# One scatter for two experts, one-hot transposes in other PSUM banks, and the low parts of the mixing weights on VectorE

## What is computed

```python
p = h @ w_in                      # pool | conv a | conv b | q k v | z | decay, beta | gates
y_pool = pool_mixer(...)          # causal means over 2, 4, 8, 16 tokens, mapped 128 -> 256 per group
y_conv = silu(layer_norm(causal_depthwise(glu, w_dw) + b_dw)) @ w_conv_out      # 31 taps
y_dn   = gated_rmsnorm(gated_delta_chunked(q, k, v, g, beta, S0), z) @ w_dn_out # q, k, v: 4 taps, silu
mixed  = gates0 * y_pool + gates1 * y_conv + gates2 * y_dn
x = layer_norm(ALPHA * x + mixed @ w_out)
x = layer_norm(ALPHA * x + ffn(x))                  # layer 0: swiglu; layer 1:
    vals, idx = lax.top_k(x @ w_router + b_router, 2); wts = softmax(vals)
    out = sum over e of gate[:, e] * swiglu(x, wg[e], wu[e], wd[e])
```

## Time and profile before

| what | us |
|---|---|
| median of 3 runs | 1764.94 (1764.79 to 1766.91) |
| the profiled execution, whole | 1761.52 |
| its span, first to last instruction | 1759.7 |
| mixing stage of layer 0, to the layer norm | about 5 to 453 |
| dense feed-forward | about 468 to 710 |
| mixing stage of layer 1 | about 724 to 1178 |
| experts, to the last add | about 1207 to 1736 |

### The profile page before, as it was taken

One profiled execution on the slowest core, in us unless ns is written; L12 is line 12 of the kernel. 1 busy time (PEld: TensorE's weight loads), 2 busy tenths in 40 slices (PEclk: granted clock), 3 DMA queues, 4 the chain that ended last, 5 costly groups with the idle time before them and its releaser, 6 DMA issues.

```text
span 1759.7 us, 22898 instructions
## 1 busy us (share of the span) xinstructions
PE 1555.0 (88%) x8707; PEld 1361.5 (77%) x8707; DVE 1153.0 (66%) x1564; ACT 813.4 (46%) x1352; POOL 828.7 (47%) x414
## 2 busy tenths in 40 slices
PE   7798888899799999688988898888999899899885
PEld 6687787787699999567888788765878778778774
DVE  6779786557611011686979844855787688688774
ACT  4544443532333243353534434322666566567653
POOL 4457565426376667343756642440343244234332
PEclk9999899989899999898998997996999999999987
DMA  5222223312355453322222332233687588588771
GB/s 230 96 96 75 70 72 101 144 48 90 121 165 160 130 159 106 123 72 96 77 85 81 95 127 72 72 133 114 217 324 291 199 308 304 200 301 306 262 253 41
DMA packets 57523, 264.66 MB, mean 150 GB/s; under 512 B 9024, under 2 KB 9664, under 8 KB 48448
## 3 DMA queue, kind: packets, MB, share of 16 engines
q1 hardware_dynamic: 57408, 263.11, 43.3%
HBM read 254.54 MB, written 8.54 MB: 150 GB/s over the span
## 4 chain that ended last, share of the span: by engine, by line
PE 47%; DVE 29%; POOL 10%; issue 9%; ACT 4%; DMA 1%; POOLq 0%; ACTq 0%; DVEq 0%; SPq 0%
POOL fl L528 7%; PE ps L1320 6%; PE ps L1321 6%; PE ps L1322 6%; DVE cacc L1565 6%; PE ps L1025 5%; PE ps L1026 4%; PE ps L1027 4%; PE ps L1293 3%; DVE ml L1907 2%; DVE kT L1473 2%; DVE qT L1473 2%; DVE pw L1538 1%; DVE G L1810 1%; POOL ml L592 1%
## 5 line engine op out<-in xcount | busy, mean ns | idle before, releaser
L548 POOL TENSOR_TENSOR Wl<-raw,Wh 128x1024 fp32r<-128x1024 f32 x138 | 344.5, 2500 | 351.3 <-ACT Wh L619 351.0
L1025 PE MATMUL ps<-Xh,Wl 128*128 128x320 f32 x976 | 335.0, 343 | 49.1 <-POOL Wl L548 31.4
L1907 DVE TENSOR_TENSOR ml<-mraw,mh 128x1408 fp32r<-128x1408 f32 (+1 forms) x160 | 299.4, 1892 | 105.1 <-ACT mh L910 104.5
L592 POOL TENSOR_TENSOR ml<-mraw,mh 128x1408 fp32r<-128x1408 f32 (+1 forms) x56 | 184.9, 3302 | 363.5 <-ACT mh L910 363.5
L910 ACT ACTIVATE mh<-mraw 128x1408 fp32r<-128x1408 f32 (+1 forms) x216 | 268.4, 1252 | 112.5 <-PE ps L1322 109.1
L1026 PE MATMUL ps<-Xl,Wh 128*128 128x320 f32 x976 | 314.1, 322 | 0.0
L1027 PE MATMUL ps<-Xh,Wh 128*128 128x320 f32 x976 | 313.8, 322 | 0.0
L1025 PEld LDWEIGHTS ps<-Xh,Wl 128*128 128x128 f32 x976 | 195.5, 200 | 76.3 <-POOL Wl L548 43.1
L528 POOL TENSOR_TENSOR fl<-fraw,fh 128x1024 fp32r<-128x1024 f32 (+1 forms) x60 | 158.8, 2652 | 88.2 <-ACT fh L857 88.2
L1026 PEld LDWEIGHTS ps<-Xl,Wh 128*128 128x128 f32 x976 | 195.6, 200 | 0.3
L1027 PEld LDWEIGHTS ps<-Xh,Wh 128*128 128x128 f32 x976 | 194.6, 199 | 0.0
(11 more groups left out here) (336 smaller groups left out, 3151.7 us busy)
## 6 DMA issues: line engine op xcount, KB each, us to landing
mraw<-w_moe SPq DMA_DIRECT2D x128, 704.0 KB, 6.3
raw<-w_mix SPq DMA_DIRECT2D x68, 1024.0 KB, 4.9
mraw<-w_moe SPq DMA_DIRECT2D x88, 512.0 KB, 4.3
fraw<-w_ffn SPq DMA_DIRECT2D x44, 512.0 KB, 3.5
fraw<-w_ffn SPq DMA_DIRECT2D x16, 704.0 KB, 4.0
Ss<-st_delta SPq DMA_DIRECT2D x2, 2048.0 KB, 9.1
o_delta_s<-Ss SPq DMA_DIRECT2D x8, 512.0 KB, 2.6
X<-x SPq DMA_DIRECT2D x2, 640.0 KB, 5.7
```

The source lines that it names most:

```text
L548: pool.tensor_tensor(Wl[:, n % 3, :], raw[:, b % 3, u % 2, :], Wh[:, n % 3, :].bitcast(f32), ALU.subtract).then_inc(w_lo, 1)
L592: pool.tensor_tensor(ml[:, n % MS, 0:w], mraw[:, n % MRAW, 0:w], mh[:, n % MS, 0:w].bitcast(f32), ALU.subtract).then_inc(m_lop, 1)
L1025: pe.matmul(out, wl, xh, start=start, stop=False)
L1907: dve.tensor_tensor(ml[:, n % MS, 0:w], mraw[:, n % MRAW, 0:w], mh[:, n % MS, 0:w].bitcast(f32), ALU.subtract).then_inc(m_lod, 1)
```

## The change

Three things are changed.

1. The low part `Wl` of every mixing unit is made by DVE (`wrest`) in place of POOL (`rest`), at the same place of the list `STEPS`. For the first two units of layer 1 both halves stand ahead of the layer norm's own work, and the first two units of layer 0 stand between the splits of X. POOL keeps its share of the taps, the sums and the other low parts.
2. The results of experts 2p and 2p + 1 stay in two sets of `yh` and `yl`, and one scatter adds both in PSUM (four matmuls per block in place of two), spread over tiles 3 to 10 of expert 2p + 2. DVE adds 32 blocks in place of 64.
3. The slot weights of a pair are made once, after tile 2 of the even expert, in PS[3], and both one-hot transposes after tile 2 of the odd expert, in PS[3] and PS[4], the banks of the up tiles. PE waits for their copies by ACT ahead of tile 8.

```diff
 # experts, ACT
-                    act.wait_ge(m_ptc, e + 1)
+                    if e >= 2:
+                        act.wait_ge(m_sc, 8 * (e // 2))
...
-                    if i == 7 + SCAT:
-                        act.wait_ge(m_pt, e + 1)
-                        act.activation(gslot[:, :], PS[6][:, T:T + 1], ACT.Copy)
-                        act.activation(PT[:, :], PS[6][:, 0:T], ACT.Copy).then_inc(m_ptc, 1)
+                    if i == 4 and e % 2 == 0:
+                        act.wait_ge(m_gs, e // 2 + 1)
+                        act.activation(gslot[:, e:e + 2], PS[3][:, 0:2], ACT.Copy).then_inc(m_ptc, 1)
+                    if i == 4 and e % 2:
+                        act.wait_ge(m_pt, e // 2 + 1)
+                        for j in range(2):
+                            act.activation(PT[:, j, :], PS[3 + j][:, 0:T], ACT.Copy).then_inc(m_ptc, 1)
 # experts, PE
+                def slots(e):
+                    if e:
+                        pe.wait_ge(m_tlo, 3 * e)
+                    pe.wait_ge(m_p, e + 2)
...
+                def places_turned(e):
+                    pe.wait_ge(m_tlo, 3 * e)
...
-                def scatter(e, m):
+                def scatter(pair, m):
                     if m == 0:
-                        pe.wait_ge(m_ylo, 2 * e + 2)
-                        pe.wait_ge(m_ptc, e + 1)
-                    else:
-                        pe.wait_ge(m_acc, e * 8 + max(m - 1, 0))
+                        pe.wait_ge(m_ylo, 4 * pair + 4)
+                        pe.wait_ge(m_ptc, 3 * pair + 3)
+                    elif m > 1:
+                        pe.wait_ge(m_acc, 8 * pair + m - 1)
                     c = slice(128 * m, 128 * m + 128)
-                    pe.matmul(PS[6 + m % 2][:, 0:T], yl[:, c], PT[:, :], start=True, stop=False)
-                    pe.matmul(PS[6 + m % 2][:, 0:T], yh[:, c], PT[:, :], start=False, stop=True).then_inc(m_sc, 1)
+                    o = PS[6 + m % 2][:, 0:T]
+                    for j in range(2):
+                        pe.matmul(o, yl[j][:, c], PT[:, j, :], start=(j == 0), stop=False)
+                        ins = pe.matmul(o, yh[j][:, c], PT[:, j, :], start=False, stop=(j == 1))
+                    ins.then_inc(m_sc, 1)
...
                         else:
+                            if k == MG:
+                                pe.wait_ge(m_ptc, 3 * (e // 2) + (3 if e % 2 else 1))
                             wide(e * MN + k, PS[3:6], FUNIT, *fed(k - MG), k == MG, False)
-                        if k >= SCAT and e:
-                            scatter(e - 1, k - SCAT)
-
-                    pe.wait_ge(m_p, 2 * (e // 2) + 2)
-                    pe.wait_ge(xt_dve, 6)
-                    if e:
-                        pe.wait_ge(m_acc, e * 8)
...
+                        if k == 2:
+                            if e % 2:
+                                places_turned(e)
+                            else:
+                                slots(e)
+                        if k >= SCAT and e and e % 2 == 0:
+                            scatter(e // 2 - 1, k - SCAT)
 # experts, DVE
-                    if SCAT <= i < SCAT + 8 and e:
-                        add(e - 1, i - SCAT)
+                    if SCAT <= i < SCAT + 8 and e and e % 2 == 0:
+                        add(e // 2 - 1, i - SCAT)
 # mixing, POOL
-            def rest(n):
...
-                rest(l * NU)
-                rest(l * NU + 1)
...
-                        if p == 0 and u < U_WO + 6:
-                            rest(l * NU + u + 2)
 # mixing, DVE
             def ln(l, w):
...
+                if w == 2:
+                    wrest((l + 1) * NU)
+                    wrest((l + 1) * NU + 1)
...
+            def wrest(n):
...
+                dve.wait_ge(w_hi, n + 1)
+                dve.tensor_tensor(Wl[:, n % 3, :], raw[:, b % 3, u % 2, :],
+                                  Wh[:, n % 3, :].bitcast(f32), ALU.subtract).then_inc(w_lo, 1)
...
             def part(l, u, p):
+                if p == 0 and u < U_WO + 6:
+                    wrest(l * NU + u + 2)
```

More of the change, by code:

```diff
@@ L115, in build @@
             ("gate", [128, 3, NE + 1], f32), ("posm", [128, 3, NE + 1], f32),
-            ("gslot", [128, 1], f32), ("flag", [128, 1], mybir.dt.int32))
+            ("gslot", [128, NE], f32), ("flag", [128, 1], mybir.dt.int32), ("warm", [1, 1], f32))
+        SQAT = sum(size(s) for s in ([1, NCON], [1, DEPTH, NPAR], [1, KT, T], [1, KT, T], [1, KT, T], [1, 3, 2, UNIT],
+                                     [1, 3, UNIT], [1, 3, UNIT], [1, KT, 8]))
         (G, EXT) = lay(TOP, ("G", [128, 24, T], f32))
@@ L568, in _ @@
                 for kind, x in STEPS:
-                    if kind == "part":
-                        u, p = x
-                        if p == 0 and u < U_WO + 6:
-                            rest(l * NU + u + 2)
-                    elif kind == "ptap":
+                    if kind == "ptap":
                         tap(l, *x)
@@ L593, in _ @@
                                            mh[:, n % MS, 0:w].bitcast(f32), ALU.subtract).then_inc(m_lop, 1)
-                    sums(m_acc, 8 * (NE - 1), asum, KT - 1)
+                    sums(m_acc, 4 * NE - 8, asum, KT - 1)
                     with pool.If(overflow(pool)):
@@ L735, in ln @@
                 src = (None, X, acc)[w]
-                act.activation(std[0:1, 0:1], C("ones", 1), ACT.Sqrt)
+                if w == 2:
+                    head((l + 1) * NU)
+                    head((l + 1) * NU + 1)
+                act.activation(warm[:, :], C("ones", 1), ACT.Sqrt)
                 for m in range(k):
@@ L748, in ln @@
                     return
[L749 to L752, removed]
+                if w == 1 and l == 0:
                     fhead(0, 0)
                     fhead(0, 1)
-                else:
+                elif w == 1:
                     mhead(0)
@@ L939, in y_head @@
                     act.wait_ge(m_done, (e + 1) * MN)
-                    act.wait_ge(m_ptc, e + 1)
+                    if e >= 2:
+                        act.wait_ge(m_sc, 8 * (e // 2))
                     for c in range(2):
-                        act.activation(yh[:, 512 * c:512 * c + 512], PS[6 + c][:, :], ACT.Copy, scale=gslot[:, 0:1])\
+                        act.activation(yh[e % 2][:, 512 * c:512 * c + 512], PS[6 + c][:, :], ACT.Copy, scale=gslot[:, e:e + 1])\
                             .then_inc(m_yhi, 1)
@@ L1367, in experts @@
                         pe.wait_ge(m_p, 2 * (e // 2) + 4)
+                        pe.wait_ge(m_ylo, 2 * e)
+                        pe.wait_ge(m_acc, 8 * (e // 2))
                         gather_next(e, 0)
[L1369 removed]
                         gather_next(e, 1)
@@ L1389, in experts @@
                 for m in range(8):
-                    scatter(NE - 1, m)
+                    scatter(NE // 2 - 1, m)
             def ffn(l):
@@ L1940, in y_rest, with add @@
                         s = slice(512 * c, 512 * c + 512)
-                        dve.scalar_tensor_tensor(out=yl[:, s], in0=PS[6 + c][:, :], scalar=gslot[:, 0:1],
-                                                 in1=yh[:, s].bitcast(f32), op0=ALU.mult, op1=ALU.subtract).then_inc(m_ylo, 1)
-                def add(e, m):
-                    dve.wait_ge(m_sc, e * 8 + (m + 1))
+                        dve.scalar_tensor_tensor(out=yl[e % 2][:, s], in0=PS[6 + c][:, :], scalar=gslot[:, e:e + 1],
+                                                 in1=yh[e % 2][:, s].bitcast(f32), op0=ALU.mult, op1=ALU.subtract).then_inc(m_ylo, 1)
+                def add(pair, m):
+                    dve.wait_ge(m_sc, 8 * pair + m + 1)
                     dve.tensor_tensor(acc[:, m, :], acc[:, m, :], PS[6 + m % 2][:, 0:T], ALU.add).then_inc(m_acc, 1)
@@ L1993, in experts @@
                 for m in range(8):
-                    add(NE - 1, m)
-                dve.wait_ge(m_acc, 8 * NE)
+                    add(NE // 2 - 1, m)
+                dve.wait_ge(m_acc, 4 * NE)
             for m in range(KT):
@@ L1999, in _ @@
                 dve.tensor_tensor(Xl[:, m, :], X[:, m, :], Xh[:, m, :].bitcast(f32), ALU.subtract).then_inc(split_lo, 1)
+                if m % 4 == 3:
+                    wrest(m // 4)
             dve.wait_ge(par_in, 16)
```

54 lines of the change are left out of this document (28 added, 26 removed).

## The result

The changed kernel takes 1664.46 us (median of 4, 1656.22 to 1667.15) beside 1765.93 us for the kernel before on the same chip: a ratio of 0.9416, 95% interval 0.9383 to 0.9448. The profiled executions differ by 94.3 us in span (1759.7 and 1665.4).

What follows compares the result with a forecast made beforehand. No single engine was taken to bound the kernel: POOL's `Wl` holds DVE, and late adds pause PE and halve its clock. Mixing stages -39 and experts -35 sum to -74, a median of 1691 us, range 1665 to 1727.

Steps and rivals of the forecast that it cites:

- What bounds the kernel: Whole kernel: pace passes between engines; PE's idle time could give 205 us; POOL's `Wl` stops DVE some 2 us.
- q, k, v units: Units at each layer's start: without the hold PE becomes the slower engine; -11 us in layer 0, -14 in layer 1.
- First delta steps: Units 14, 15 and 17: `Wl` and a wait for `Wh` stand ahead of steps PE needs; +1 us per layer.
- Woven part: 100 to 300 us in layer 0: `Wl` cost 33, waits for `Wh` at half, holds -49; -3 us per layer.
- Branches: End of the branches, 340 to 450 us: holds of 18.9 us go, 16 `Wl` cost 18; -5 us per layer.
- Experts: Pair scatter and moved transposes: -25 waits, -20 half clock, +8 remaining pauses, +2 tail; -35 us.
- the tail: End of the experts: the last pair's 8 blocks of four matmuls at half clock end some 2 us later.
- the residual: Even experts: `ml` may still delay an `add` before a block; three pauses of the longest kind, 8 us.
- A: Rival, woven part: waits for `Wh` block DVE while delta steps queue; +12 per layer, not -3; 1721 us; chance 0.15.
- B: Rival, experts: they keep their idle, paced by DVE, loads or two-expert blocks; -5, not -35; 1721 us; chance 0.11.
- C: Rival, mixing stages: `Wl` on DVE and POOL's taps hold each other up, mixing gains nothing; 1730 us; chance 0.06.
- D: Rival, slower: from the woven part on each `Wl` and `Wh` wait lies on the path; 1780 us; chance 0.04.

Runs made afterwards that it cites:

- experiment 6: The changed kernel, but DVE makes `Wl` only for units 0 to 13 of each layer and POOL makes the other 55: 1694.9 us.
- experiment 2: The kernel before with `Wl` made by DVE and the high parts ahead of the norm, experts unchanged: 1713.15 us.
- experiment 3: The changed kernel without pairs: one scatter per expert, 64 adds, each transpose after the expert's third tile in PS[4]: 1663.28 us, ratio 0.9422.
- experiment 4: The changed kernel with the pair scatter, but slot weights and transposes behind tile 10 in PS[6] and PS[7]: 1683.4 us.
- experiment 5: The changed kernel with one wait put back: in experts 2, 4 and 6 PE waits behind tile 10 for the pair's last add: 1670.27 us.

## Why the prediction was off

**What bounds the kernel.** Right. The hold of DVE by POOL's `Wl`, the last add ahead of the transposes, and the half clock behind a pause were the three causes, and each came up in the experiments. The size was not: the median came 26.5 us under the forecast of 1691. 20.3 of them are the difference of the profiled spans (94.3 measured, 74 forecast), 13 in the experts and 7 in the mixing stages. The other 6 are scatter: the profiled execution of the kernel before lay 3.4 us under its median, that of the changed kernel 2.7 above its own. The 7 of the mixing stages are small by luck, since the woven parts gave 17 us more than forecast and the start of layer 1 and the branches 10 less.

**q, k, v units.** Layer 0: -11 forecast, -10.6 measured. PE is the slower engine, as forecast: most of its units take 4.35 to 4.67 us, and it has no wait over 0.2 us between them up to 69.6. The activations were not 4.3 to 4.5 us apart, though. Two steps took 8.94 and 8.58, in which DVE waited for ACT, and six took 3.74, DVE's own time (3.8 was worked out), with which it caught up. Layer 1: -14 forecast, -10.2 measured. The units gave 9.3, and the start about 1 in place of 4.5. The two operations on X fell from 4.04 to 1.01 us as forecast, but the norm's `std` by ACT ahead of them was only 18.6 us earlier in a kernel that was 21.2 ahead at the end of layer 0's branches; the two `Wl` that stand before it on DVE are 3.0 us of work there. And the third tile came no sooner, because ACT's high part of it waits for its load:

```profile
715.06 1.06 ACT L610 ACTIVATE Wh<-raw 128x1024 fp32r<-128x1024 f32 x1 [6.44 <-DMA raw<-w_mix]
```

It stood at 736.04 before, behind 6.07 us of the same wait, so it moved by 21.0 us. PE still waits 3.8 us for that tile's `Wl`, where it waited 4.60. No run tested an earlier load.

**First delta steps.** +1 forecast in each layer; +2.5 measured in layer 0 and -0.1 in layer 1.

**Woven part, the first step that failed.** The step is "I count a wait at half: -3 per layer" (by its own terms, 33 + 12 - 49, it would be -4). The part gave 13 us in layer 0 and 10 in layer 1. Units 20 to 52 of layer 0 in the kernel before:

```profile
119.50:338.30 218.80, 189.45 (x1287) 179.41 (x1286) 170.68 (x250) 97.43 (x223) 132.11 (x90) 0.95 0.28 93
```

Beside the row of the changed kernel in experiment 6, PE is busy as long as before, 189.5 us, and idles 16.8 in place of 29.4: the whole gain is idle time of PE. DVE is busy 9.3 us less; 32 `Wl` at 1.14 came in, so holds of 45.8 us went. 20.5 us of waits for `Wh` came in, while DVE's other idle time fell from 48.1 to 24.5. The prediction had counted 31 us of idle time, over 100 to 300, and charged half of each wait. In this account of DVE's busy and idle time, its ledger, the waits took the place of other idle time entirely. The ledger does not price a wait, though: taking waits away afterwards gave 0.7 us for each. Both stand together only if freeing DVE of the holds was worth more than the 45.8 us that the held operations lasted too long. The reading is that PE, which waited for a held delta step, let DVE wait for its next product in turn, so that this idle time of DVE was the hold's as well. It rests on the ledger and on experiment 6, where PE's idle time came back with the hold (from 17 to 27 us); it was not isolated. What failed is thus the sum itself, which priced the holds at their length and the waits at half.

**Branches.** -5 per layer forecast; 0.0 and -4.1 measured. In layer 0 PE's idle time fell from 11.1 to 6.3 us, but the clock from 0.88 to 0.83, and the busy time rose by as much. That differs from one execution to the next. Six profiled executions have this same mixing stage: the changed kernel twice and experiments 2 to 5. PE idled 6.3 to 7.4 us in the stretch in all six, but it took 98.9 us in three and 94.4 to 95.6 in the others, with 34.1 us at half clock in the first three and 20.5 to 27.3 in the others. So the change gave 3 to 5 us here in three executions and nothing in the other three.

**Experts, the larger failure.** The mechanism was right, and the sum had -25 for idle time, -20 for clock, +8 for pauses left over and +2 for the tail. Measured were -24.7, -23.9, 0 and +1.4. The clock was sized low because the mean clock by stretch had given 44 us at half and 20 was taken where 22 followed; the clock's record has 47.8. The step that failed is the residual: "in even experts `ml` may still delay an `add` before a block", priced at three pauses of the longest kind. Such a block waits for the add two blocks earlier. No such wait is left inside the experts of the changed kernel, nor in experiment 3 with the adds of the kernel before. The waits of 2.7 us needed two groups of `Pm` operations held one after the other (3.26 and 3.59 us), and in the changed kernel and in experiments 3 and 4 the second group no longer fell beside an `ml` of POOL (0.67 us). What sets how the two engines meet there was not tested and stays open.

**The pair scatter.** The prediction credited the change as a whole. Experiment 3 shows that the moved transposes bring all of it. Its experts took 2.3 us more without the pairs in the profiled execution, 1.7 of which are clock, and the medians show no difference.

**The rivals.** A fell for the change as a whole, though its mechanism is real: some 22 us could still be had from the waits for `Wh`. B fell: DVE ran at 81% with loads at 0.78 in experiment 3 without holding PE up. C fell: the mixing stages gained 46 us where they were to gain nothing, and `Wl` on DVE took 1.22 us in the median and 1.89 at most. The 141 us that it gave to POOL's taps were taps and `Wl` together; without `Wl` POOL is busy 62 of 206 us in that part. The Trainium skill's sentence (Perfetto Trace Analysis, "Optimizing Scalar/DVE Operations") that offloading between the two engines might not help is not borne out here in that direction: experiment 2, from POOL to DVE, gained 52 us, since the same subtraction takes mostly 2.35 to 2.8 us on POOL and 1.14 from start to start on DVE. DVE's `Wl` does hold POOL in turn: a tap beside one took up to 1.95 us, where the median of all is 0.88. D did not come near.

## What to carry to other kernels

Ask of a late operation who waits for it: the last adds were 2.4 us late in the kernel before and in experiment 3 alike, and moving the one waiter to other banks gave 50 us, while halving the adds gave nothing on top. Price an operation of POOL on SBUF operands by what it does to DVE beside it, and compare DVE's busy and idle time over the same work, not over the same time; then look at PE's idle time, since here the gain was larger than DVE's own. And when an operation moves to an engine that works in order, place it where its input is ready: half a unit later was worth 22 us.

## What was not expected of the hardware

Three pauses of TensorE of 1.3 to 1.4 us in a busy stretch left the clock at 1.00 (experiment 5). In experiment 4 two of 2.2 us and one of 1.3 were followed by 3.4 to 6.8 us at 0.50, as those of 3.1 us were in the kernel before. So one of 3.1 us cost up to 6.5, and one of 1.4 only itself. A POOL tap of about 1 us stretched DVE operations too, among them `Wl`, which took 1.15 to 1.89 us (median 1.22). The same instructions can meet a different clock from one execution to the next: the branches of layer 0 had 20.5 to 34.1 us at half clock in six executions and took 94.4 to 98.9 us.
